# Inverse sums moved out of the transpose ring in prompt attention, and row transposes of the routed experts regrouped for the next pair

## The reference

```python
# prompt attention, per block of 128 queries and per head (both kinds end like this)
s = scale * q @ k.T            # masked, the sparse half also with a bias
p = jax.nn.softmax(s, axis=-1)
o = p @ v

# routed experts: tokens sorted by expert, in padded blocks; XB rows are gathered tokens
xb = x_pad[slot_token].reshape(n_blocks, blk, D)
yb = lax.map(lambda a: swiglu(a[0], w_e_gu[a[1]], w_e_down[a[1]]), (xb, block_expert))
def swiglu(x, w_gu, w_down):
    g, u = jnp.split(x @ w_gu, 2, axis=-1)
    return (jax.nn.silu(g) * u) @ w_down
```

## Time and profile before

| | us |
|---|---|
| median of 3 runs | 3026.5 (3021.57 to 3031.03) |
| profiled execution | 3026.11 |
| its span, first to last instruction | 3024.2 |
| PE busy | 2623.8 (87%) |
| DVE busy | 1517.7 (50%) |
| ACT busy | 1107.1 (37%) |
| prompt attention on TensorE | about 1399 to 1757 |
| routed experts on TensorE | about 2099 to 2923 |

### The profile page before, as it was taken

One profiled execution on the slowest core, in us unless ns is written; L12 is line 12 of the kernel. 1 busy time (PEld: TensorE's weight loads), 2 busy tenths in 40 slices (PEclk: granted clock), 3 DMA queues, 4 the chain that ended last, 5 costly groups with the idle time before them and its releaser, 6 DMA issues. The chain is left out here.

```text
span 3024.2 us, 43954 instructions
## 1 busy us (share of the span) xinstructions
PE 2623.8 (87%) x14542; PEld 1465.3 (48%) x14542; DVE 1517.7 (50%) x3765; ACT 1107.1 (37%) x2376; POOL 371.5 (12%) x415
## 2 busy tenths in 40 slices
PE   4798996859989899896989969797989899999978
PEld 0344443628878687774556634444333233333323
DVE  0256555377868777784887655485111111111116
ACT  0223221458969678782644511121111111111111
POOL 0000000111001010101122122043000000000025
PEclk8899998979999899995999989898999999999988
DMA  9422113522236021206110064215989888897867
GB/s 386 159 60 75 48 58 99 231 76 90 70 111 224 18 102 36 88 1 173 33 26 24 9 230 139 103 52 209 394 312 397 312 323 331 303 364 257 298 232 303
DMA packets 243832, 510.72 MB, mean 169 GB/s; under 512 B 24021, under 2 KB 102047, under 8 KB 236240
## 3 DMA queue, kind: packets, MB, share of 16 engines
q1 hardware_dynamic: 196388, 328.73, 31.5%
q0 software_dynamic: 28352, 126.04, 11.3%
q10 hardware_dynamic: 18932, 53.91, 4.6%
HBM read 630.82 MB, written 87.01 MB: 237 GB/s over the span
## 5 line engine op out<-in xcount | busy, mean ns | idle before, releaser
L2852 PE MATMUL routed_ex_pG<-dispatch_exWG,routed_ex_XT 128*64 128x512 f32 x2048 | 473.6, 605 | 24.6 <-DVE routed_ex_XT L2943 13.0
L1995 DVE TENSOR_REDUCE ssqc<-SQ 128x8 f32<-128x512 f32 x516 | 346.1, 682 | 126.4 <-ACT SQ L1798 113.1
L1709 PE MATMUL eK<-dWkv,LT 128*128 128x256 f32 x1032 | 318.5, 391 | 12.3 <-ACT SQ L1798 11.8
L1712 PE MATMUL eK<-WA,LT 128*128 128x272 f32 x1032 | 328.5, 401 | 0.0
L2943 DVE COPY routed_ex_XT<-routed_ex_pX 128x512 f32<-128x512 f32 x128 | 85.6, 689 | 474.6 <-PE routed_ex_pX L2839 474.5
L1798 ACT ACTIVATE SQ<-eK 128x512 f32<-128x512 f32 x516 | 291.9, 602 | 58.0 <-PE eK L1712 42.0
L549 PE MATMUL in_pp<-ada_Win,in_hT 128*128 128x512 f32 (+1 forms) x640 | 282.0, 599 | 9.8 <-ACT in_pr L463 9.8
L2852 PEld LDWEIGHTS routed_ex_pG<-dispatch_exWG,routed_ex_XT 128*64 128x64 f32 x2048 | 137.2, 138 | 272.3 <-issue 249.1
L2871 PE MATMUL routed_ex_pY<-routed_ex_WD,routed_ex_AT 128*64 128x512 f32 x1024 | 233.3, 596 | 9.1 <-DMA routed_ex_WD<-in_w_e_down 7.4
L1712 PEld LDWEIGHTS eK<-WA,LT 128*128 128x128 f32 x1032 | 201.8, 196 | 29.0 <-DVE numc L1994 0.2
L1709 PEld LDWEIGHTS eK<-dWkv,LT 128*128 128x128 f32 x1032 | 191.2, 197 | 47.8 <-ACT SQ L1798 17.0
(11 more groups left out here) (546 smaller groups left out, 3757.2 us busy)
## 6 DMA issues: line engine op xcount, KB each, us to landing
dispatch_exWG<-in_w_e_gu SPq DMA_DIRECT2D x256, 1024.0 KB
routed_ex_WD<-in_w_e_down SPq DMA_DIRECT2D x132, 1024.0 KB, 13.7
s_yblk<-routed_ex_Y ACTq DMA_DIRECT2D x64, 512.0 KB
ada_Wada<-in_w_ada SPq DMA_DIRECT2D x8, 3072.0 KB, 17.1
s_yblk<-zrows SPq DMA_DIRECT2D x15, 1024.0 KB
ada_Win<-in_w_in ACTq DMA_DIRECT2D x4, 2048.0 KB, 13.8
dispatch_exWG<-in_w_e_gu SPq DMA_DIRECT2D x4, 2048.0 KB, 18.9
s_tdT<-in_td SPq DMA_DIRECT2D x8, 832.0 KB
```

Source lines behind the costliest of these rows:

```text
L1709: pe.matmul(pK[kn % 3][:, 512 + z:512 + z + HK], key, Wkv[:, 4:8, 0:NOPE], start=True, stop=True)
L1712: pe.matmul(pK[kn % 3][:, z:z + HK + 16], key, WA[:, pr, :], start=True, stop=True).then_inc(s_KN, 1)
L1995: dve.tensor_reduce(ssqc[cg % 2][:, n - 1 - tau, :], SQ[kn % 4].rearrange("p (h d) -> p h d", h=H), AX.X, ALU.add).then_inc(s_red, 1)
L2852: m = pe.matmul(pG[u][r, :], XT[u][:, k, r], WG[2 * u + v][:, k, :], start=(k == 0), stop=(k == KD - 1))
```

## The change

Two edits that do not touch each other.

In prompt attention the inverse sums leave the ring `pT`: `inverse_sums(n-1)` now runs on TensorE after `turn(n)`, and writes columns 128 to 255 of the output bank that item n-1 does not use. It waits for the normalisation of item n-2, which reads that bank. ScalarE takes them out (`take_inverse`) after the evacuations of `turn(n)` instead of before them. In `pv` the multiplications by V come first and the side work for the sample tokens after them; VectorE's `norm` waits for both.

In the routed experts each pair now transposes the rows of the next pair. The first pair's rows are transposed ahead of the loop (`turn_first`); inside a pair all four `gate_up` calls follow one another, and then, per block, `turn_a(u)` and the 8 transposes of the next pair's block stand together ahead of `down(u, 0)` and `down(u, 1)`. POOL fetches rows for the next pair, and the list has two more columns for the block pair after the last. The counts of the semaphores follow.

```diff
@@ stage attend, TensorE
-                    if a < 0:
-                        pe.wait_ge(s_rs, n)
-                        for b in range(2):
-                            m = pe.matmul(pT[x % 2][64 * b:64 * b + 64, 0:P], rs[:, (n - 1) % 2, b:b + 1].to_broadcast([P, 64]), c("ident"), start=True, stop=True)
...
+            def inverse_sums(n):
+                pe.wait_ge(s_rs, n + 1)
+                if n >= 1:
+                    pe.wait_ge(s_on, n)
+                for b in range(2):
+                    m = pe.matmul(pO[(n + 1) % 2][64 * b:64 * b + 64, P:2 * P], rs[:, n % 2, b:b + 1].to_broadcast([P, 64]), c("ident"), start=True, stop=True)
+                m.then_inc(s_inv, 1)
...
             def pv(n):
-                if n >= 2:
-                    pe.wait_ge(s_on, n - 1)
+                for j in range(i + 1):
+                    for a in range(2):
+                        m = pe.matmul(pO[n % 2][64 * a:64 * a + 64, 0:P], V[g][:, j, h * 64:h * 64 + 64], PT[n % 2][a][:, j, :],
...
                 elif 0 <= n - CHUNK0 < len(chunks):
+                    m.then_inc(s_O, 1)
                     pe.wait_ge(s_zb, k + 1)
...
                 turn(n)
                 if n:
+                    inverse_sums(n - 1)
                     pv(n - 1)
@@ stage attend, ScalarE and VectorE
+            def take_inverse(n):
+                act.wait_ge(s_inv, n + 1)
+                if n >= 2:
+                    act.wait_ge(s_on, n - 1)
+                act.activation(RB[n % 2][:, :], pO[(n + 1) % 2][:, P:2 * P], ACT.Copy).then_inc(s_inve, 1)
             for n in range(NI + 1):
                 evac(act, n, False)
+                if n:
+                    take_inverse(n - 1)
                 if n + 1 < NI:
                     exps(n + 1)
...
             def norm(n):
                 dve.wait_ge(s_O, n + 1)
+                if 0 <= n - CHUNK0 < len(chunks):
+                    dve.wait_ge(s_zm, n - CHUNK0 + 1)
                 read_sums(n)
-                evacuated(dve, gfirst[n + 1] + 1)
+                dve.wait_ge(s_inve, n + 1)
@@ stage_routed, TensorE
+                def turn_next(u):
+                    b, ahead = 2 * (1 - q) + u, 2 * q + 2 + u
+                    pe.wait_ge(s_x[b], i * 16 + (16 * q + 16))
+                    for n in range(2):
+                        pe.wait_ge(s_xe, i * 8 + (2 * ahead + n + 1))
+                        for k in range(4):
+                            m = pe.transpose(pX[n][:, k * P:(k + 1) * P], X[b][:, (4 * n + k) * P:(4 * n + k + 1) * P], c("ident"))
+                        m.then_inc(s_xt, 1)
...
-                turn_x(0, 0)
-                turn_x(0, 1)
-                gate_up(0, 0)
-                turn_x(1, 0)
-                gate_up(0, 1)
-                turn_x(1, 1)
-                gate_up(1, 0)
-                turn_a(0)
-                gate_up(1, 1)
-                down(0, 0)
-                turn_a(1)
-                down(0, 1)
-                down(1, 0)
-                down(1, 1)
+                for u in range(2):
+                    for n in range(2):
+                        gate_up(u, n)
+                for u in range(2):
+                    turn_a(u)
+                    turn_next(u)
+                    for n in range(2):
+                        down(u, n)
+
+            for u in range(2):
+                turn_first(u)
             run(pe, pair)
@@ stage_routed, ScalarE and VectorE
                 sigmoid(0)
-                take_a(0)
                 sigmoid(1)
-                take_y(0, 0)
-                take_a(1)
-                take_y(0, 1)
-                take_y(1, 0)
-                take_y(1, 1)
+                for u in range(2):
+                    take_a(u)
+                    for n in range(2):
+                        take_y(u, n)
...
+                for u in range(2):
+                    for n in range(2):
+                        dve.wait_ge(s_xt, i * 8 + (4 * q + 4 + 2 * u + n + 1 + XT0))
+                        dve.wait_ge(s_gu, n0 + u + 1 + GU0)
+                        take_x(u, n)
```

More of the change, by code:

```diff
@@ L168, in build @@
         G["nblk"] = sb("nblk", [1, 2], I32)
-        G["list"] = sb("list", [P, NBLK], I32)
+        G["list"] = sb("list", [P, NBLK + 2], I32)
         G["pages"] = sb("pages", [P, NS // 2], I32)
@@ L1004, in turn @@
                         evacuated(pe, x - 1)
[L1005 to L1013 removed]
+                    pe.wait_ge(s_P, n + 1)
+                    for b in range(cnt):
+                        m = pe.transpose(pT[x % 2][:, b * P:(b + 1) * P], S[n % 2][a][:, (b0 + b) * P:(b0 + b + 1) * P], c("ident"))
+                    m.then_inc(s_T, 1)
+            def inverse_sums(n):
[5 more added lines that the diff above has]
+                m.then_inc(s_inv, 1)
             def pv(n):
@@ L1039, in pv @@
                     m.then_inc(s_zm, 1)
+                    return
                 elif n == FOLD:
                     pe.wait_ge(s_zl, 1)
-                    pe.matmul(pO[0][0:32, 384:512], c("fold32"), zparts[:, :, :].rearrange("p n w -> p (n w)"), start=True, stop=True)
+                    m = pe.matmul(pO[0][0:32, 384:512], c("fold32"), zparts[:, :, :].rearrange("p n w -> p (n w)"), start=True, stop=True)
                 elif n == TURN:
@@ L1045, in pv @@
                     for a in range(2):
-                        pe.transpose(pO[0][:, 384 + 16 * a:400 + 16 * a], zld[a], c("ident")[0:16, 0:16])
-                for j in range(i + 1):
-                    for a in range(2):
-                        h = 2 * p + a
-                        m = pe.matmul(pO[n % 2][64 * a:64 * a + 64, 0:P], V[g][:, j, h * 64:h * 64 + 64], PT[n % 2][a][:, j, :],
-                                      start=(j == 0), stop=(j == i))
+                        m = pe.transpose(pO[0][:, 384 + 16 * a:400 + 16 * a], zld[a], c("ident")[0:16, 0:16])
                 m.then_inc(s_O, 1)
@@ L2747, in _ @@
             dve.wait_ge(s_lt, 1)
-            link(dve.tensor_copy(G["list"][:, :], pL))
+            link(dve.memset(G["list"][:, NBLK:NBLK + 2], 0))
+            link(dve.tensor_copy(G["list"][:, 0:NBLK], pL))
             for m in (NT - 1, NT):
@@ L2828, in _, with turn_first @@
                 pe.sem_inc(s, start)
+            def turn_first(u):
+                pe.wait_ge(s_x[u], 16)
+                for n in range(2):
+                    pe.wait_ge(s_xe, 2 * u + n + 1)
+                    for k in range(4):
+                        m = pe.transpose(pX[n][:, k * P:(k + 1) * P], X[u][:, (4 * n + k) * P:(4 * n + k + 1) * P], c("ident"))
+                    m.then_inc(s_xt, 1)
             def pair(i, q):
                 n0 = i * 4 + 2 * q
-                def turn_x(u, n):
-                    if n == 0:
-                        pe.wait_ge(s_x[2 * q + u], i * 16 + 16)
-                    pe.wait_ge(s_xe, (n0 + u) * 2 + n + 1)
-                    for k in range(4):
-                        m = pe.transpose(pX[n][:, k * P:(k + 1) * P], X[2 * q + u][:, (4 * n + k) * P:(4 * n + k + 1) * P], c("ident"))
-                    m.then_inc(s_xt, 1)
+                def turn_next(u):
+                    b, ahead = 2 * (1 - q) + u, 2 * q + 2 + u
+                    pe.wait_ge(s_x[b], i * 16 + (16 * q + 16))
+                    for n in range(2):
+                        pe.wait_ge(s_xe, i * 8 + (2 * ahead + n + 1))
+                        for k in range(4):
+                            m = pe.transpose(pX[n][:, k * P:(k + 1) * P], X[b][:, (4 * n + k) * P:(4 * n + k + 1) * P], c("ident"))
+                        m.then_inc(s_xt, 1)
                 def gate_up(u, n):
```

56 lines of the change are left out of this document (28 added, 28 removed).

## The result

The changed kernel takes 2974.64 us (median of 4 runs, 2973.05 to 2977.59) against 3026.7 (4 runs, 3021.57 to 3031.03) measured beside it. The ratio is 0.9834, 95% interval 0.982 to 0.9847: 52 us less, where 47 were forecast (27 + 20).

| stretch | before | after | difference | forecast |
|---|---|---|---|---|
| up to the first scores of prompt attention | 1399.45 | 1400.18 | +0.7 | 0 |
| prompt attention, first scores to last `norm` | 357.92 | 328.44 | -29.5 | -20 |
| from there to the first row transpose | 341.38 | 338.89 | -2.5 | 0 |
| first row transposes to the first sigmoid | 11.99 | 13.48 | +1.5 | +1.5 |
| 31 periods of the routed experts | 794.65 | 770.48 | -24.2 | -29.8 |

A forecast was written before the change was run, and what follows sets the result against it. TensorE's list was taken to bound 20 routed-expert periods, the weight stream 11; in prompt attention TensorE paced 44 of 64 items. Routed experts -27 and attention -20 (-11 - 3 - 6) took 3026.1 to 2979, median 2980; range 2956 to 3004.

The forecast's parts named there:

- Free period: Routed experts: a pair paced by TensorE's list falls from 24.79 to 23.30 us, 0.98 from shape changes, 0.51 from XT.
- Late periods: Routed experts: in 11 of 31 periods weights set the end and gain 0; the other 20 gain 29.8 us.
- rival 1: Routed experts: the weight stream takes more, ten periods at DMA share 0.86 turn late; gain 12 us, kernel 2994; chance 0.19.
- Start and end: Routed experts: extra transposes ahead of the loop cost 1.5 us, those of the last pair 1.4 us.
- rival 1's other form: Routed experts: the 0.16 us belongs to register instructions, also between gate_up calls; gain 12 us, same time 2994.
- Prompt attention, steps: Fewer shape changes save 0.35 us in 32 items, 0.15 in 32; 16 us, of which 11 count.
- choice of 0.15 for split scores: Prompt attention: 32 items with 64*128 scores keep one shape change before transposes, saving 0.15 us each, not 0.35.
- rival 4: TensorE's clock falls to 1.2 GHz in more pairs; four give 3070 us; chance 0.07 together with no gain.
- the order of the side work: Prompt attention: pv running first hides part of the 12.1 us wait for POOL; 6 us, between 0 and 12.
- Ring: Prompt attention: pT has one group less an item, so transposes stop waiting for the sums' copy; 3 us of 3.4.
- Rival 2: Prompt attention: VectorE takes over and only 3 us are left of the gain; kernel 2996; chance 0.11.
- Rival 3: Both stages mostly give their upper bounds, -43 in routed experts and -30 in prompt attention; kernel 2953; chance 0.07.

The follow-up runs named there:

- t_transpose: The changed kernel with one dummy 128x128 transpose between two gate_up calls of every pair; free period 23.80 us against 23.39.
- x_side: The kernel before with only prompt attention's side work moved behind the multiplications by V; 3013.78 us, ratio 0.9964.
- x_routed: The kernel before with the whole edit of the routed experts and nothing of prompt attention; 3005.39 us, ratio 0.994.
- x_ahead: The changed kernel with the inverse sums ahead of the transposes, still in the output bank, and copied ahead of the evacuations; 2990.88 us, ratio 0.9886.
- x_sums: The kernel before with only the inverse sums moved behind the transposes, into the other output bank; 3016.04 us, ratio 0.9975.
- t_matmul: The changed kernel with two dummy 128*64 matmuls of 128 columns between two gate_up calls of every pair; free period 23.60 us against 23.39.
- one_burst: The changed kernel with one burst of 20 transposes per routed pair instead of two of 10; 2970.67 us, ratio 0.9825.
- n_before: The kernel before with half of each later expert's weight load left out, results wrong; 2997.44 us, executed once.
- n_after: The changed kernel with half of each later expert's weight load left out, results wrong; 2928.22 us, executed once.

## Why the prediction was right, and where it was off

1. **Free period.** Forecast 23.30, measured 23.39. The term that was mis-sized is the change of shape: 6 changes at 0.15 us are 0.90, not 0.98. The prediction's own rows had 0.14 to 0.16 left over, and it took the upper end. The 0.51 for `XT` fits what is left (0.90 + 0.51 = 1.41 of the 1.40).
2. **Late periods.** This is the step that was wrong in its count. The 11 periods "in which the weights set the end" were whole windows of the earlier trace rows; one by one only 5 were late, and 26 free. All 26 would have gained 36.4 us (26 x 1.40), but four turned late, all four with a DMA share of 1.04 before. The extra excess, 45.4 - 26.1 = 19.3 us, stands where 11 x 1.49 = 16.4 was left out, so two errors of count came close to each other, and that -24.2 lies near -29.8 is partly luck. One of the four lies in the window at 0.86, which is rival 1 for one period in ten. That the bytes of the weights take it, the two kernels with half the weights show.
3. **Start and end** +1.5 and +1.0, about as reckoned, though the start holds a wait of 0.76 us for the copy to `XT` that had no term. No wait for `AT`; rival 1's other form, the register instructions, fell with the `gate_up` run of 64, which has them inside, and with `t_transpose`, which pays 0.30 us without one.
4. **Prompt attention, steps** -29.5 against -20 in all, inside the bounds of -7 to -38. The step between shapes was 0.30 and 0.15 us an item, where 0.35 and 0.15 stood. The choice of 0.15 for split scores held. The Trainium skill, "TensorEngine Tiling (Array Packing)", Key Properties, says that a new tiling mode drains the engine while another tile of the same mode does not; the rows agree for columns and now for rows: 64\*128 scores still pay ahead of a 128\*128 transpose (0.21 us left over), 96\*128 ones do not (0.10).
5. **Prompt attention, what was too small.** Two terms. Query blocks 0 and 1, priced by steps alone, gave 10.1 of the 29.5 us, by a shorter stretch at 1.2 GHz; no term stood for the clock as a gain, only rival 4 as a loss. And the order of the side work was put at 6 us, half of the wait for `zB`, because VectorE was taken to be level in half of these items. `x_side` has 10.9 us less of that wait than `x_routed` and takes 12.0 us less in blocks 3 to 6: nearly all of the wait reached the end. In the changed kernel 5.6 us of it are left, where under 3 was the sign. Besides, the side work's own shape was left out, so that the two edits of attention looked separate.
6. **Ring.** The 3 us for the ring are not seen: `x_ahead` frees the ring as well, and takes 202.8 us in blocks 3 to 6 as `x_side` does, which keeps it.
7. **Rival 2** fell: VectorE still waits, 22.9 us. But it has come closer: TensorE's waits for VectorE's maxima rose from 4.4 us to 10.1. **Rival 3** came half true, in attention alone. **Rival 4** fell: no free period lost its clock in either kernel. The Trainium skill, "TensorE: Matmul & The Clock Gate", Part 4: PE-mode transpose, says that transposes don't count as busy for the clock in the same way; here bursts of 20, 2.3 us between matmuls, left it at 1.00 in the free periods, and no experiment made a longer one.

The total came out closer than its parts: attention gave 10 us more than forecast and the periods 6 us less, and the two partly cancel. That is luck.

Left open: why the 1.2 GHz stretch at the start of prompt attention ends where it does. In five kernels with the sums ahead of the transposes it ended near 1440, in eight with the sums behind them at 1412 to 1427 (in `x_sums` with 3 us of full clock inside it; in `t_matmul` 7 us of 1.2 GHz came back at 1439). That is a regularity, not a cause. Seven of those eight have the same prompt attention to the letter, and it took 325.3 to 328.5 us in them.

## What to carry over

Count changes of the array's shape on TensorE's list as instructions of their own, in the order in which they will stand after all edits: a short piece of a third shape can undo what two other pieces gained by standing together. Where a stage alternates between a full instruction list and a late stream, read both period by period, not by windows, and expect periods near a DMA share of 1.00 to turn late as the list gets shorter. Where the engine runs at the lower clock in a stretch, a change there is worth more than its steps, in either direction, and the range should say so.

## What the runs showed of the hardware

- A change between a 128\*64 matmul and a 128\*128 transpose costs 0.15 us at 2.4 GHz (0.30 for two in `t_transpose`, 0.30 for two less in `one_burst`). Items of prompt attention are 0.15 us shorter for each change less when changes between 128\*32 and 128\*64 are counted too, and 64\*128 scores ahead of a 128\*128 transpose leave 0.21 us over, 96\*128 ones 0.10.
- The DMA queues, mostly weights, moved 403 and 404 GB/s over single periods, and 336 GB/s over the whole stage in after, 337 in `one_burst`, 325 before.
- In the routed experts the granted clock fell below 1.00 only in late periods, behind a time in which TensorE stood for weights (windows of 0.94 to 0.97 in after; 0.89 in the 31.56 us period of `one_burst` with a stand of 5.3 us). In `n_before` and `n_after`, where no period is late, it did not fall between the first and the last sigmoid, with the bursts of transposes of before and after.
